# Unread products of a constant ahead of a sublayer's first products, and around a mixer's back-turn, in a two-part transformer block on one core

## The chip, the cores and the metric

The kernel runs on one core of one Trainium2 chip. The metric is device time in microseconds, the median of the runs shown.

## The reference

Two blocks follow each other on 256 tokens of width 1024, all in float32. The first has two layers of feed-forward, mixer, feed-forward; the second has two layers of attention and a routed mixture of experts. Every sublayer starts with a norm and a modulation of the tokens, and its first products need that result.

```python
def modulate(x, g_pre, shift, scale):
    return rms_norm(x, g_pre) * (1 + scale) + shift

for l in range(DEPTH):                       # DEPTH = 2, first block
    mod = (c_act @ ada_w[l] + ada_b[l]).reshape(bsz, N_SUB, 3, D_MODEL)[:, :, :, None, :]
    h = modulate(x, norm_pre[l, 0], mod[:, 0, 0], mod[:, 0, 1])
    x = residual_add(x, swiglu(h, ffn_w_gate[l, 0], ffn_w_up[l, 0], ffn_w_down[l, 0]), ...)
    h = modulate(x, norm_pre[l, 1], mod[:, 1, 0], mod[:, 1, 1])
    y = token_mixer(h, mix_w_in[l], ...)     # ends: merged = sum of gated branches; merged @ w_out
    x = residual_add(x, y, ...)
    h = modulate(x, norm_pre[l, 2], mod[:, 2, 0], mod[:, 2, 1])
    x = residual_add(x, swiglu(h, ffn_w_gate[l, 1], ...), ...)

for i in range(DEPTH):                       # second block
    h = rms_norm_2(x, norm_mix_g[i]) * (1.0 + sc1) + sh1
    y = diff_attention(h, ...) if i % 2 == 0 else chunked_attention(h, ...)
    x = x + g1 * y
    h = rms_norm_2(x, norm_ffn_g[i]) * (1.0 + sc2) + sh2
    x = x + g2 * grouped_moe(h, ...)
```

## The kernel before

Tokens lie on the 128 partitions in two tiles. A plan (`make_plan`) lists steps in order: norm, ffn or mixer or heads, resid, and in the mixers also backT and out. Each engine walks through the plan and issues its own instructions in the order in which the code stands; semaphores tie the engines together. TensorE's queue is in order, so what waits there holds everything behind it.

Weights arrive as chunks of 1 MB in a ring (`stage<-wstream`). ScalarE rounds each chunk to its high part (`w_hi`, L667), VectorE takes the rest (`w_lo`, L1181). A product in full precision is three matmuls (`mm3`, L1978, L1981, L1982): high by high, high by low, low by high, with 512 columns as a rule. The normed input is split in the same way into `hT_hi` and `hT_lo`.

A norm goes in four rounds, two for each token tile, and each handles half the width. For one round ScalarE scales the tokens (`tok`, L1087), TensorE transposes four blocks of 128 (`norm_round`, L1994) into one of two `tr` banks, VectorE applies the modulation (`tf`, L1838), ScalarE makes `hT_hi` (L1104) and VectorE makes `hT_lo` (L1847). A sublayer's first products are interleaved with the norm by `first_columns` (L2005): twelve matmuls of the first tile on the first half of the width, round 2's transposes, twelve on the second half, round 3's transposes, then twice twelve for the second tile. Rounds 0 and 1 stand before it in the queue. `first_columns` is called in seven places: in three feed-forwards (the second, third and fourth; they write to `gu`), in both mixers and in both heads sublayers (they write to `acc`; in the mixers with 416 columns). The first feed-forward does it another way.

At the end of a mixer the gated and summed branches lie in `tok`, tokens on partitions. The step backT turns them back: four calls of `turn` (L2076) with four transposes each, after a wait for VectorE's last sum (`mg_ready`, L1734). ScalarE (L745) and VectorE (L1207) copy each round's result into `hT_hi` and `hT_lo`, and rounds 2 and 3 wait until the banks of 0 and 1 are free. The step out multiplies by `w_out`.

`ident` is a 128x128 part of the table `const`, a constant in SBUF. `gu` (two banks), `acc` (four) and `tr` (two) are the PSUM banks.

Of the kernel before, what the change touches and what calls it, by code (L numbers as in the profile page):

```python
# [286 lines left out]
def build(nc, wstream, ada_stream, c_in, xin, const_in, vec_in, bgate_in, lam_in, rbias_in, t5_in, rel_in, rw_in, out):  # L287
# [14 lines left out]
    with ExitStack() as ctx:  # L302
        def sb(name, shape, dt=F32):
            return ctx.enter_context(nc.sbuf_tensor(name, shape, dt))
# [57 lines left out]
        const = sb("const", [P, N_CONST])  # L362
# [24 lines left out]
        acc = ctx.enter_context(nc.psum_tensor("acc", [P, 4, 512], F32))  # L387
        gu = ctx.enter_context(nc.psum_tensor("gu", [P, 2, 512], F32))
# [76 lines left out]
        def cst(name):  # L465
            return const[:, CONST[name][0]:CONST[name][1]]
# [36 lines left out]
        ident, ones, tri = cst("ident"), cst("ones"), cst("tri")  # L503
# [1471 lines left out]
        def _(pe):  # L1975
# [21 lines left out]
            def normed(b, part):  # L1997
# [4 lines left out]
                    pe.wait_ge(tr_free, b["u"] - 1 + part + 2 * t)  # L2002
                return ready

            def first_columns(b, dst, width=512):  # L2005

                for t in range(NT):
                    for part in range(2):
                        r = 2 * t + part
                        pe.wait_ge(tr_free, b["u"] - 1 + r)  # L2010
                        columns(b["n"] + part, dst, 4 * part, 4, part == 0, part == 1, width, only=(t,))
                        if t == 0:
                            norm_round(b["u"] - 4, b["tf"] - 4, 2 + part, b["src"] - 4)
# [53 lines left out]
            def turn(u, srcs, i=0, per=0, scaled=None):  # L2067

                if scaled is None:  # L2070
                    pe.wait_ge(tr_free, u + 1 + per * i)
                else:
                    pe.wait_ge(tf_ready, scaled)
                for j, src in enumerate(srcs):
                    rows_ = src.shape[-1]
                    ins = pe.transpose(tr[0:rows_, u % 2, j * P:(j + 1) * P], src, ident)  # L2076
                ins.then_inc(tr_full, 1)
# [566 lines left out]
            for step, b in plan:  # L2644
# [18 lines left out]
                elif kind == "mixer":  # L2663
                    mixer(b, step[1])
                elif kind == "backT":
                    pe.wait_ge(mg_ready, b["mg"])
                    for r in range(4):
                        turn(b["u"] + r, [tok[:, t, (2 * r + k) * P:(2 * r + k + 1) * P] for k in range(2) for t in range(NT)])
                elif kind == "out":
                    def of(c):  # L2670
# [16 lines left out]
                elif kind == "route":  # L2687
# [25 lines left out]
                    bank, sent, before = acc[:, 0, :], rt[:, 3, :], cst("before")  # L2713
# [180 lines left out]
```

## Time and profile before

| | us |
|---|---|
| median of 3 runs | 2193.05 |
| lowest, highest | 2189.24, 2195.68 |
| profiled execution | 2198.06 |
| its span, first to last instruction | 2196.2 |
| TensorE busy | 1993.8 |
| VectorE busy | 1423.0 |
| ScalarE busy | 841.4 |
| mean granted TensorE clock | 0.969 |

The profile is of one execution. A timeline row gives start, duration, engine, line and operation, output and inputs by their names, shapes, and in brackets the idle time before it and what ended it. Matmuls are pipelined: a row's end is later than the moment at which the next can start. The granted clock is a share of TensorE's full speed; it has two levels, 1.00 (2.4 GHz) and 0.50 (1.2 GHz). "issue" stands where the profile names no releaser.

### The profile page before, as it was taken

To read this page: it belongs to the slowest core of one execution; us is meant where nothing else is said; L and a number is where in the kernel's file an instruction comes from. 1 tells how busy PE (TensorE), PEld (TensorE's weight loads), DVE (VectorE), ACT (ScalarE), POOL (GpSimd) and SP (SyncE) were. 2 spreads that over 40 slices of the span, in tenths; PEclk is the share of its full clock that TensorE was granted. 3 is DMA by queue.
4 is the path that set the end of the run, shared out by engine and by line. 5 is a ranking of instruction groups with operands and counts; after the bars stand their busy time and mean duration, and the time that the engine had idled before them with its cause. 6 is when DMAs were issued, how large, how long until landed. Compare 5 with 4: busy or idle time off the path is not lost.

```text
span 2196.2 us, 26289 instructions
## 1 busy us (share of the span) xinstructions
PE 1993.8 (91%) x9588; PEld 1457.0 (66%) x9588; DVE 1423.0 (65%) x2167; ACT 841.4 (38%) x1101; POOL 65.2 (3%) x93
## 2 busy tenths in 40 slices
PE   3999899999999999899999999976899879879987
PEld 2788777777887788777777887755544347654432
DVE  6888787767888799677766888776311157642111
ACT  3333545655444444555655334542100035320000
POOL 0000000000000000000000000111000011000000
PEclk9999999999999999999999999997999989989999
DMA  9999454427996899453426897433799975359997
GB/s 396 363 364 361 163 189 155 145 96 296 359 375 243 321 369 380 165 181 141 168 96 249 347 374 293 151 127 109 288 422 422 421 316 183 99 200 410 420 421 310
DMA packets 98175, 597.87 MB, mean 272 GB/s; under 512 B 20240, under 2 KB 23696, under 8 KB 27408
## 3 DMA queue, kind: packets, MB, share of 16 engines
q1 hardware_dynamic: 91600, 585.18, 67.9%
q10 hardware_dynamic: 6464, 11.15, 1.5%
q8 instruction: 76, 1.25, 0.2%
q14 instruction: 35, 0.29, 0.0%
HBM read 595.21 MB, written 1.09 MB: 272 GB/s over the span
## 4 chain that ended last, share of the span: by engine, by line
PE 58%; DMA 15%; DVE 15%; ACT 5%; issue 5%; POOL 1%; SPq 1%; DVEq 0%; ACTq 0%; POOLq 0%
PE acc L1978 9%; PE acc L1982 9%; PE acc L1981 9%; PE gu L2327 8%; DMA proj<-ada_stream 7%; PE tr L2327 5%; DVE w_lo L1181 5%; DMA w_raw<-wstream 4%; PE gu L1978 4%; PE gu L1982 4%; PE gu L1981 4%; PE tr L2076 2%; PE acc L2327 2%; DMA stage<-wstream 2%; DVE proj L1239 2%
## 5 line engine op out<-in xcount | busy, mean ns | idle before, releaser
L1181 DVE TENSOR_TENSOR w_lo<-stage,w_hi 128x2048 fp32r<-128x2048 f32 x233 | 532.5, 2289 | 85.1 <-ACT w_hi L667 84.3
L667 ACT ACTIVATE w_hi<-stage 128x2048 fp32r<-128x2048 f32 x233 | 444.6, 1912 | 236.7 <-PE acc L1982 233.1
L1239 DVE SCALAR_TENSOR_TENSOR proj<-proj,c_row 128x1024 f32<-128x1024 f32 x240 | 291.9, 1220 | 56.5 <-DMA proj<-ada_stream 45.9
L1978 PE MATMUL acc<-w_hi,hT_hi 128*128 128x512 f32 (+1 forms) x736 | 307.5, 418 | 20.6 <-DVE hT_lo L1847 12.2
L1978 PE MATMUL gu<-w_hi,hT_hi 128*128 128x512 f32 x704 | 284.8, 404 | 21.3 <-DVE pair L1309 10.5
L1982 PE MATMUL acc<-w_hi,hT_lo 128*128 128x512 f32 (+1 forms) x736 | 292.7, 398 | 0.0
L1981 PE MATMUL acc<-w_lo,hT_hi 128*128 128x512 f32 (+1 forms) x736 | 292.6, 398 | 0.0
L1982 PE MATMUL gu<-w_hi,hT_lo 128*128 128x512 f32 x704 | 278.8, 396 | 0.0
L1981 PE MATMUL gu<-w_lo,hT_hi 128*128 128x512 f32 x704 | 278.5, 396 | 0.0
L1978 PE MATMUL acc<-w_hi,yT_hi 128*128 128x512 f32 (+1 forms) x460 | 181.3, 394 | 2.7 <-ACT proj L961 2.7
L1978 PEld LDWEIGHTS acc<-w_hi,hT_hi 128*128 128x128 f32 x736 | 143.3, 195 | 58.5 <-DVE hT_lo L1847 15.5
L1982 PE MATMUL acc<-w_hi,yT_lo 128*128 128x512 f32 (+1 forms) x460 | 179.3, 390 | 0.0
L1981 PE MATMUL acc<-w_lo,yT_hi 128*128 128x512 f32 (+1 forms) x460 | 179.1, 389 | 0.0
L2327 PE MATMUL gu<-stage,got 128*64 128x512 f32 x736 | 163.6, 594 | 14.7 <-DMA stage<-wstream 14.7
L1978 PEld LDWEIGHTS gu<-w_hi,hT_hi 128*128 128x128 f32 x704 | 134.8, 191 | 53.0 <-DVE pair L1309 13.0
L1982 PEld LDWEIGHTS acc<-w_hi,hT_lo 128*128 128x128 f32 x736 | 142.3, 193 | 30.7
L1981 PEld LDWEIGHTS acc<-w_lo,hT_hi 128*128 128x128 f32 x736 | 143.3, 195 | 25.7
L1982 PEld LDWEIGHTS gu<-w_hi,hT_lo 128*128 128x128 f32 x704 | 134.6, 191 | 29.5
L1981 PEld LDWEIGHTS gu<-w_lo,hT_hi 128*128 128x128 f32 x704 | 135.0, 192 | 26.7
L2327 PEld LDWEIGHTS gu<-stage,got 128*64 128x64 f32 x736 | 57.1, 137 | 117.5 <-issue 104.2
L1396 DVE TENSOR_TENSOR pair<-pair,gu 128x256 f32<-128x256 f32 x32 | 13.5, 421 | 169.6 <-ACT pair L806 169.6
L2327 PE MATMUL tr<-w_raw,hidT 128*64 128x512 f32 x512 | 114.3, 595 | 4.7 <-DVE got L1379 3.0
(230 smaller groups left out, 2278.7 us busy)
## 6 DMA issues: line engine op xcount, KB each, us to landing
stage<-wstream SPq DMA_DIRECT2D x332, 1024.0 KB, 5.9
proj<-ada_stream SPq DMA_DIRECT2D x120, 1024.0 KB, 7.8
w_raw<-wstream SPq DMA_DIRECT2D x96, 1024.0 KB, 16.7
tok<-gate_rows SPq DMA_DIRECT2D x10, 512.0 KB, 4.1
tf<-bgate_in ACTq DMA_DIRECT2D x12, 256.0 KB, 3.3
proj<-rel_in ACTq DMA_DIRECT2D x16, 192.0 KB, 2.4
z_mix<-wstream SPq DMA_DIRECT2D x2, 1024.0 KB, 17.6
once<-wstream SPq DMA_DIRECT2D x2, 1024.0 KB, 25.6
```

Source lines behind the costliest of these rows:

```text
L667: act.activation(w_hi[:, n % PARTS, :], stage[:, n % STAGES, :], ACT.Copy).then_inc(hi_ready, 1)
L1181: dve.tensor_tensor(w_lo[:, n % PARTS, :], stage[:, n % STAGES, :], w_hi[:, n % PARTS, :].bitcast(F32), ALU.subtract).then_inc(chunk_ready, 1)
L1239: ins = dve.scalar_tensor_tensor(w, w, 1.0, c_row[:], ALU.mult, ALU.mult, accum_out=dst)
L1396: dve.tensor_tensor(both[:, j, BLK:2 * BLK], both[:, j, 0:BLK], gu[:, j, BLK:2 * BLK], ALU.mult).then_inc(both_ready, 1)
L1978: ins = pe.matmul(dst, l_hi, r_hi, start=start, stop=False, skip_group_check=True)
L1981: pe.matmul(dst, l_hi, r_lo, start=False, stop=False, skip_group_check=True)
L1982: return pe.matmul(dst, l_lo, r_hi, start=False, stop=stop, skip_group_check=True)
L2076: ins = pe.transpose(tr[0:rows_, u % 2, j * P:(j + 1) * P], src, ident)
L2327: return pe.matmul(dst, lhs, rhs, start=start, stop=stop, skip_group_check=True)
```

## The change

A helper `unread` issues f32 matmuls of 128x512 with `ident` as the stationary and the first 512 columns of `const` as the moving operand. Their result is not read: the next real product into that bank starts it anew. Four stand in `first_columns`, before its first wait and into the bank of the second token tile. In backT two stand before the wait for the last sum, and two between rounds 1 and 2, all into `gu`.

```diff
+            def unread(bank, times):
+
+                for _ in range(times):
+                    pe.matmul(bank, ident, const[:, 0:512], start=True, stop=True, skip_group_check=True)
+
             def first_columns(b, dst, width=512):
 
                 for t in range(NT):
                     for part in range(2):
                         r = 2 * t + part
+                        if r == 0:
+                            unread(dst(1) if width == 512 else acc[:, 1, :], 4)
                         pe.wait_ge(tr_free, b["u"] - 1 + r)
                         columns(b["n"] + part, dst, 4 * part, 4, part == 0, part == 1, width, only=(t,))
                         if t == 0:
...
                 elif kind == "backT":
+                    unread(gu[:, 0, :], 2)
                     pe.wait_ge(mg_ready, b["mg"])
                     for r in range(4):
+                        if r == 2:
+                            unread(gu[:, 0, :], 2)
                         turn(b["u"] + r, [tok[:, t, (2 * r + k) * P:(2 * r + k + 1) * P] for k in range(2) for t in range(NT)])
```

In TensorE's queue the back-turn of a mixer stands as follows before. L1982 is the last product of the branches, `tr<-const,tok` are the transposes, the rows below belong to the step out.

```order
L1982 MATMUL acc<-w_hi,yT_lo 128x512
L2076 MATMUL tr<-const,tok 128x128 x16
L1978 MATMUL acc<-w_hi,hT_hi 128x512
L1981 MATMUL acc<-w_lo,hT_hi 128x512
L1982 MATMUL acc<-w_hi,hT_lo 128x512
```

In the same place after the change (lines are seven further down from `turn` on):

```order
L1982 MATMUL acc<-w_hi,yT_lo 128x512
L2008 MATMUL gu<-const 128x512 x2
L2083 MATMUL tr<-const,tok 128x128 x8
L2008 MATMUL gu<-const 128x512 x2
L2083 MATMUL tr<-const,tok 128x128 x8
L1978 MATMUL acc<-w_hi,hT_hi 128x512
```

The sixteen transposes are cut into two groups of eight with two products in front of each. At the start of the second feed-forward TensorE's queue holds, before (transposes of rounds 0 and 1, then the first products):

```order
L1982 MATMUL acc<-w_hi,hT_lo 128x512
L1994 MATMUL tr<-const,tok 128x128 x8
L1978 MATMUL gu<-w_hi,hT_hi 128x512
L1981 MATMUL gu<-w_lo,hT_hi 128x512
L1982 MATMUL gu<-w_hi,hT_lo 128x512
```

and after:

```order
L1982 MATMUL acc<-w_hi,hT_lo 128x512
L1994 MATMUL tr<-const,tok 128x128 x8
L2008 MATMUL gu<-const 128x512 x4
L1978 MATMUL gu<-w_hi,hT_hi 128x512
L1981 MATMUL gu<-w_lo,hT_hi 128x512
L1982 MATMUL gu<-w_hi,hT_lo 128x512
```

Only the four products are new there. The queues of the other engines hold the same rows in the same order as before.

## Rows read from the trace of the kernel before

**Rows 1.** The page: busy time of TensorE, share of the span, instructions.

```profile
PE 1993.8 (91%) x9588; PEld 1457.0 (66%) x9588; DVE 1423.0 (65%) x2167; ACT 841.4 (38%) x1101; POOL 65.2 (3%) x93
```

**Rows 2.** Waits of TensorE: waiting tile and line, releaser: us, times, longest.

```profile
PE acc L1978 <- DVE hT_lo L1847: 12.2, 8, 2.6
```

**Rows 3.** Timeline, TensorE: start, us, instruction, shapes; f32 products in the first mixer.

```profile
411.37 1.14 PE L2327 MATMUL acc<-soft_p,const 128*128 128x128 f32 x6
412.27 0.48 PE L1978 MATMUL acc<-w_hi,hT_hi 128*128 128x512 f32 x1
```

**Rows 4.** Chain of waits, second feed-forward: start, us, piece; the last pieces at each clock.

```profile
515.21 0.43 PE gu L1981
...
516.87 0.23 PE gu L1981
```

**Rows 5.** Timeline, TensorE: back-turns of both mixers, and the next norm after each.

```profile
481.21 1.09 PE L2076 MATMUL tr<-const,tok 128*128 128x128 f32 x8 [1.50 <-DVE tok L1734]
...
484.02 1.25 PE L2076 MATMUL tr<-const,tok 128*128 128x128 f32 x8 [1.71 <-DVE hT_lo L1207]
...
507.47 1.27 PE L1994 MATMUL tr<-const,tok 128*128 128x128 f32 x8 [0.40 <-ACT tok L1087]
...
1145.46 1.09 PE L2076 MATMUL tr<-const,tok 128*128 128x128 f32 x8 [1.51 <-DVE tok L1734]
...
1148.27 1.97 PE L2076 MATMUL tr<-const,tok 128*128 128x128 f32 x8 [1.71 <-DVE hT_lo L1207]
...
1174.31 1.27 PE L1994 MATMUL tr<-const,tok 128*128 128x128 f32 x8 [0.40 <-ACT tok L1087]
```

**Rows 6.** Busy time by stretch: PE, PEld, DVE, ACT, POOL; PEclk, DMA share, GB/s.

```profile
478.00:490.00 12.00, 8.78 (x46) 6.89 (x45) 9.54 (x10) 4.08 (x5) 0.00 (x0) 1.00 0.04 1
...
1147.30:1154.10 6.80, 5.83 (x18) 4.97 (x19) 4.29 (x6) 2.99 (x3) 0.00 (x0) 0.50 0.07 1
```

**Rows 7.** Timeline, TensorE, then ScalarE and VectorE: start of the second feed-forward.

```profile
511.43 0.47 PE L1978 MATMUL gu<-w_hi,hT_hi 128*128 128x512 f32 x1 [2.69 <-issue]
...
515.84 0.60 PE L1994 MATMUL tr<-const,tok 128*128 128x128 f32 x4
...
516.38 0.50 PE L1978 MATMUL gu<-w_hi,hT_hi 128*128 128x512 f32 x1
...
514.50 1.33 ACT L1087 ACTIVATE tok<-x_tok,rs 128x512 f32<-128x512 f32 x2
...
515.64 0.68 DVE L1847 TENSOR_TENSOR hT_lo<-tf,hT_hi 128x512 fp32r<-128x512 f32 x1
```

**Rows 8.** Timeline, TensorE, then VectorE: start of the third feed-forward.

```profile
708.61 0.76 PE L1978 MATMUL gu<-w_hi,hT_hi 128*128 128x512 f32 x1 [2.69 <-issue]
...
714.19 0.47 PE L1978 MATMUL gu<-w_hi,hT_hi 128*128 128x512 f32 x1
...
712.82 0.69 DVE L1847 TENSOR_TENSOR hT_lo<-tf,hT_hi 128x512 fp32r<-128x512 f32 x1
```

**Rows 9.** Timeline, TensorE, then VectorE: start of the first heads sublayer.

```profile
1379.14 0.58 PE L1978 MATMUL acc<-w_hi,hT_hi 128*128 128x512 f32 x1
...
1377.40 0.69 DVE L1847 TENSOR_TENSOR hT_lo<-tf,hT_hi 128x512 fp32r<-128x512 f32 x1
```

**Rows 10.** Timeline, TensorE: second column half in the first mixer.

```profile
248.06 0.46 PE L1978 MATMUL acc<-w_hi,hT_hi 128*128 128x416 f32 x1 [0.45 <-DVE hT_lo L1847]
```

**Rows 11.** Timeline, then the stretch: start of the second heads sublayer.

```profile
1787.57 1.97 PE L1994 MATMUL tr<-const,tok 128*128 128x128 f32 x8 [7.01 <-ACT tok L1087]
...
1791.95 0.80 PE L1978 MATMUL acc<-w_hi,hT_hi 128*128 128x512 f32 x1 [2.40 <-DVE hT_lo L1847]
...
1796.59 0.60 PE L1994 MATMUL tr<-const,tok 128*128 128x128 f32 x4
...
1782.00:1795.80 13.80, 5.82 (x17) 4.66 (x18) 10.49 (x18) 7.92 (x16) 3.92 (x4) 0.51 0.59 240
```

**Rows 12.** Chain of waits of the third feed-forward, 700 to 905 us, by line.

```profile
by line: DMA proj<-ada_stream 32.3%; DVE w_lo L1181 17.3%; issue 8.8%; DVE proj L1239 8.3%; PE gu L1978 4.8%; PE gu L1982 4.4%; PE gu L1981 4.4%; DVE pair L1309 1.8%; PE acc L1982 1.8%; PE acc L1981 1.8%; PE acc L1978 1.7%; ACT pair L718 1.
```

## The prediction

> **What bounds the kernel now.** I read the page first: TensorE is busy for 91% of the span [rows 1]. The reader is to see that little but TensorE's own queue can set the end, so a change inside that queue counts wherever no other engine was late. Second comes the list of waits: products of the next sublayer wait for the low part of their input, hT_lo, in eight waits of up to 2.6 us [rows 2], and the three later feed-forwards have a gap of the same kind, 2.69 us [rows 7, 8]. Third, the timeline and the busy time by stretch, with the granted clock: after such a gap the clock is often at the lower of its two levels, 1.2 instead of 2.4 GHz. There a product with 512 columns takes 0.43 us, at the higher level 0.23 us [rows 4].
>
> So each seam between sublayers may cost twice: the gap, and slow products behind it. The change puts products that nobody reads into the gap. Whether the second cost counts is read from what stands next in the queue, and from when its operands are ready.
>
> **What one unread product costs.** The trace has three f32 products with a constant at full width, 128, 256 and 128 columns, together 512. They appear as six instructions, and the next product starts 412.27 - 411.37 = 0.90 us after the first [rows 3]. So each product is two instructions, 0.45 us each for 512 columns, and the 0.90 us include picking up after a wait. Without that I take 0.43 us, 0.86 a product. The other end is two instructions at 0.23 us each, 0.46. Four products are then 3.4 us, between 1.8 and 3.6. At the lower clock a product takes 1.7 us. There are 7 x 4 + 2 x 4 = 36 of them, 31 us of TensorE in all; the question is how much lies in gaps. Nothing else moves on any engine, and there is no new wait and no new DMA.
>
> **The two back-turns.** This is the largest term. The same code runs in both mixers and the trace shows both outcomes. In the first the transposes start at 481.21 and the next norm's at 507.47, 26.26 us apart; in the second at 1145.46 and 1174.31, 28.85 us apart [rows 5]. The gaps in front are the same, 1.50 or 1.51 us and twice 1.71 us. What differs is the clock: 1.00 around the first, 0.50 for 6.8 us in the second [rows 6]. The second loses 2.6 us to it. Two unread products, 1.72 us, lie in each gap. A matmul's end in the timeline is later than the engine is free (1.14 us shown in rows 3, followed after 0.90), by some 0.15 us, so there is room for about 1.65 and 1.85 us, and what sticks out is under 0.1 us. With the queue filled the clock should stay up: **-2.6 us** in the second mixer, 0 in the first.
>
> Here a rule is weighed. Around 481 us TensorE had little but sixteen transposes for some 5 us, and the clock stayed at 1.00 [rows 5, 6]. The Trainium skill says otherwise (TensorE: Matmul & The Clock Gate, Part 4: PE-mode transpose): transposes don't count as work for the clock in the way products do. By it the first back-turn should have dropped as the second did, and the change would bring 2.6 us more, 2187.1 us. The row speaks against that, at least at this point, and the sum doesn't use it.
>
> **The second feed-forward.** Transposes end at 507.47 + 1.27 = 508.74 [rows 5], the engine is free at about 508.6; unread products fill it to 512.0, which is 0.6 us past the 511.43 at which the first real one started [rows 7]. Twelve products at 0.23 us reach 514.8. Then come transposes of the second token tile, whose first half ScalarE has ready at about 515.2 (two instructions from 514.50, 1.33 us), whatever TensorE does. They end at about 515.7, and the next twelve products need hT_lo at 515.64 + 0.68 = 516.32. Before, they started at 516.38 [rows 7], though most of the first twelve had run at the lower clock. So the delay and the saving both vanish in the wait for VectorE: **-0.05 us**. The fourth feed-forward repeats this pattern, 0.
>
> **The third feed-forward.** Here all twelve ran low. hT_lo was ready at 712.82 + 0.69 = 713.51 and the products started at 714.19 [rows 8]. With a high clock unread and real products are done at 705.8 + 3.4 + 2.8 = 712.0, so hT_lo is what comes last: **-0.65 us**.
>
> **The mixers.** At 248.06 TensorE already waited 0.45 us for hT_lo, after a stretch of slow products [rows 10]; the second mixer has the same pattern. Columns are fewer (416), and the 0.6 us of delay fits as well: 0.
>
> **The first heads sublayer.** hT_lo was ready at 1377.40 + 0.69 = 1378.09, the products started at 1379.14 [rows 9]: **-1.05 us**.
>
> **The second heads sublayer.** Here the change costs. The engine had been idle for 7.01 us and the transposes ran low; the stretch to 1795.8 has a clock of 0.51 [rows 11]. The unread products start at about 1789.4 and take 1.7 us each. Before, the clock came back 3.85 us after the first product (1791.95). If it comes back as long after the first unread one, at 1793.3, then 3.9 us of low clock do 1.95 us of work, 1.5 us are left, and the twelve real products end at 1797.6 instead of 1796.59: **+1.0 us**. If it comes back at 1795.8 as before, +2.3; if earlier, near 0.
>
> **Sum.** -2.6 - 0.05 - 0.65 - 1.05 + 1.0 = -3.35 us. Against the profiled execution (2198.06 us, of which the span is 2196.2) that is 2194.7. That execution is 5.0 us above the median of the three, 2193.05, and which seams fall low differs between executions: identical back-turns did in one profile. One of two back-turns in the profile is taken as the usual share, so the same sum stands against the median: **2189.7 us**, 0.15% less.
>
> **Rivals.** (1) *All low clock is on the path.* Twelve products lose 12 x 0.20 = 2.4 us at the lower clock, a back-turn 2.6. If all seams fell low and nothing else waited: 7 x 2.4 + 2 x 2.6 = 22 us, less 7 x 0.6 for what sticks out of the gaps, -18 us, 2175 us. For it: TensorE is busy 91%, and its queue feeds the whole feed-forward behind. Against it: the readiness of hT_lo in rows 7 and 10, which no clock moves. A mild form, where other executions have both back-turns low and more full losses at the feed-forwards, gives -7 to -9 us, 2184 to 2186 us.
> (2) *The unread products don't hold the clock*, because the clock falls on something else than an empty queue. Then only delays are left: 0.6 us at six places, swallowed by waits where a wait follows, +1 to +2 us at the second heads sublayer: 2193 to 2195 us. For it: nothing shows such products in the trace. Against it: in the second feed-forward the clock came back under a row of products after the gap, with nothing else changed [rows 4, 7].
> (3) *Slower: the unread products themselves run low.* The seven places then take 6.9 us instead of 3.4 in front of the twelve real products. At the second feed-forward 508.6 + 6.9 + 2.8 = 518.3 against 515.84, +2.5 us. It decides for the worse once it happens at about four of the seven, +10 against -3, 2200 us. Against it: where I looked, at six of the seven, the queue was full until some 0.4 us before the transposes [rows 5], and only the second heads sublayer starts low.
> (4) *The gain is given back.* The third feed-forward's chain runs for 32.3% through the modulation stream's DMAs [rows 12], so its 0.65 us may be lost; so may those before it, were the stream's order not tied to the chunks that TensorE frees. It gives 2190 to 2191 us and changes no sign.
>
> **How the numbers follow.** Within 0.3% means within 6.6 us, about what a measurement of this kernel can tell from no change. My forecast together with (4) has 0.60; (1) in either form 0.20; (2) 0.12; (3) 0.06; that an execution's mix of seams shifts the median up alone 0.02. Faster by over 0.3% needs less than 2186.5: case (1) and the lucky edge of the forecast, 0.22. Slower by over 0.3%: (3) and a little, 0.07. The rest, 0.71. The range runs from the mild form of (1), 2184, to the end of (2), 2195; it leaves out the full form of (1) and (3), under 2 in 10.
>
> **What will show it.** In the profile after, the unread products appear as 72 instructions, about 0.43 us apart. Back-turns to next norm: 26.3 us in both mixers, at a clock of 1.00. In the feed-forwards the first real product starts 0.6 us later after the transposes, and the second twelve start 0.05 us after hT_lo. The second heads sublayer shows unread products at half speed. I am wrong if a low stretch still follows the seams, or if the span falls by more than 7 us, for then the products behind hT_lo were not what I took them for.

## The result, and the profile after the change

| | before | after |
|---|---|---|
| median of 14 runs each | 2193.34 us | 2196.41 us |
| lowest, highest | 2188.96, 2196.99 | 2193.82, 2199.84 |
| profiled execution | 2198.06 us | 2197.49 us |

The changed kernel takes 1.0015 times the time of the kernel before, 95% interval 1.0008 to 1.0022. That is 3 us more, where 3.35 us less was forecast, and 2196.41 us lies above the end of the range, 2195. The change is within the 0.3% that were called no change. A second series of runs gave 1.0009 [1.0000, 1.0018]. The profiled execution of the kernel before is not one of the 14 and is longer than each of them.

The page of the kernel after the change, beside [rows 1] (busy us and instructions of each engine), and its line on the DMA queue q8 (packets, MB, share of the 16 DMA engines):

```profile
PE 2012.5 (92%) x9660; PEld 1459.3 (66%) x9660; DVE 1421.6 (65%) x2167; ACT 841.5 (38%) x1101; POOL 65.1 (3%) x93
...
q8 instruction: 77, 1.26, 0.2%
```

**The seams did what was forecast.** Timeline of TensorE after the change, both back-turns and the norm behind each, which answers to [rows 5]; then the stretch that answers to the second one of [rows 6] (PE, PEld, DVE, ACT, POOL busy, granted clock, DMA share, GB/s):

```profile
477.42 1.05 PE L2083 MATMUL tr<-const,tok 128*128 128x128 f32 x8
478.30 1.88 PE L2008 MATMUL gu<-const 128*128 128x512 f32 x4
480.18 1.25 PE L2083 MATMUL tr<-const,tok 128*128 128x128 f32 x8
503.62 1.27 PE L1994 MATMUL tr<-const,tok 128*128 128x128 f32 x8 [0.40 <-ACT tok L1087]
...
1145.74 1.05 PE L2083 MATMUL tr<-const,tok 128*128 128x128 f32 x8
1146.62 1.88 PE L2008 MATMUL gu<-const 128*128 128x512 f32 x4
1148.50 1.25 PE L2083 MATMUL tr<-const,tok 128*128 128x128 f32 x8
...
1171.95 1.27 PE L1994 MATMUL tr<-const,tok 128*128 128x128 f32 x8 [0.40 <-ACT tok L1087]
```

```profile
1147.30:1154.10 6.80, 6.80 (x31) 4.84 (x30) 4.91 (x6) 3.17 (x4) 0.00 (x0) 1.00 0.07 1
```

Back-turn to norm is 26.20 us in the first mixer and 26.21 in the second, where it was 26.26 and 28.85. The clock is 1.00 in that stretch.

**Where the time went instead** is seen when each stage is measured from the first transposes of its norm to those of the next (L1994; both profiled executions, us). In brackets stands the part up to the transposes of round 3, which I call the seam:

| stage | before | after | forecast | measured |
|---|---|---|---|---|
| first mixer | 268.32 | 268.22 | 0 | -0.10 |
| second feed-forward (to round 3) | 197.18 (11.78) | 198.48 (11.76) | -0.05 | +1.30 (-0.02) |
| third feed-forward (to round 3) | 198.78 (12.38) | 201.60 (11.79) | -0.65 | +2.82 (-0.59) |
| second mixer | 270.88 | 268.25 | -2.6 | -2.63 |
| fourth feed-forward (to round 3) | 194.93 (11.75) | 194.91 (11.79) | 0 | -0.02 (+0.04) |
| first heads (to round 3) | 161.06 (12.86) | 160.13 (11.78) | -1.05 | -0.93 (-1.08) |
| second heads (to round 3) | 149.56 (12.22) | 152.02 (12.61) | +1.0 | +2.46 (+0.39) |

Every seam in brackets is within 0.06 us of its forecast, but for the second heads sublayer, which the forecast made 0.6 us too dear. The loss lies behind the seams: late in the third feed-forward, and in the second heads sublayer. The second feed-forward's +1.30 does not come back when the changed kernel is profiled again (below).

The rows of the table add up to +2.9 us, but the two profiled executions differ by -0.6. The rest is mostly the first feed-forward, 209.77 us before and 205.96 after. No unread product stands in it or ahead of it, and over the fourteen profiled executions of this study whose start is not delayed and whose transfers are full it takes 206.0 to 209.8 us. What moves it is not known; it is one reason why the medians, and not the two profiles, say how much slower the kernel is.

### The profile page after: what moved, and what is told of

It is laid out like the page before. It is cut to its first block, busy times and chain, and to the rows that moved or that the text cites. A ratio compares the mean times of both kernels' runs of the same rounds, so it can differ in the third digit from the quotient of the medians.

```text
span 2195.7 us, 26433 instructions
## 1 busy us (share of the span) xinstructions
PE 2012.5 (92%) x9660; PEld 1459.3 (66%) x9660; DVE 1421.6 (65%) x2167; ACT 841.5 (38%) x1101; POOL 65.1 (3%) x93
## 3 DMA queue, kind: packets, MB, share of 16 engines
q8 instruction: 77, 1.26, 0.2%
## 4 chain that ended last, share of the span: by engine, by line
PE 60%; DMA 15%; DVE 14%; ACT 5%; issue 4%; POOL 1%; SPq 1%; DVEq 0%; ACTq 0%; POOLq 0%
PE acc L1978 9%; PE acc L1982 9%; PE acc L1981 9%; PE gu L2334 8%; DMA proj<-ada_stream 6%; PE tr L2334 5%; PE gu L1978 4%; DVE w_lo L1181 4%; DMA w_raw<-wstream 4%; PE gu L1982 4%; PE gu L1981 4%; PE tr L2083 3%; PE acc L2334 2%; DMA stage<-wstream 2%; DVE proj L1239 2%
## 5 line engine op out<-in xcount | busy, mean ns | idle before, releaser
L1982 PE MATMUL acc<-w_hi,hT_lo 128*128 128x512 f32 (+1 forms) x736 | 290.0, 394 | 0.0
L1982 PE MATMUL gu<-w_hi,hT_lo 128*128 128x512 f32 x704 | 276.0, 392 | 0.0
L1982 PE MATMUL acc<-w_hi,yT_lo 128*128 128x512 f32 (+1 forms) x460 | 178.8, 389 | 0.0
L1982 PEld LDWEIGHTS acc<-w_hi,hT_lo 128*128 128x128 f32 x736 | 140.6, 191 | 30.3
L1981 PEld LDWEIGHTS acc<-w_lo,hT_hi 128*128 128x128 f32 x736 | 141.4, 192 | 26.2 <-issue 1.0
L1982 PEld LDWEIGHTS gu<-w_hi,hT_lo 128*128 128x128 f32 x704 | 132.7, 189 | 28.8
```

Of the source, the lines that this page charges most:

```text
L1981: pe.matmul(dst, l_hi, r_lo, start=False, stop=False, skip_group_check=True)
L1982: return pe.matmul(dst, l_lo, r_hi, start=False, stop=stop, skip_group_check=True)
```

## First series: one part at a time

**Back-turns alone.** Against the kernel before:

```diff
                 elif kind == "backT":
+                    unread(gu[:, 0, :], 2)
                     pe.wait_ge(mg_ready, b["mg"])
                     for r in range(4):
+                        if r == 2:
+                            unread(gu[:, 0, :], 2)
```

> Only the two pairs of unread products in the two back-turns are left; none stands in front of a sublayer. Theory A (the back-turns gain 1 to 2.6 us as predicted, and the loss comes from the four products in front of sublayers): 0.5 to 2.6 us faster than the kernel before, ratio about 0.999. Theory B (the back-turns' gain is given back, since the stages behind them are paced by the modulation stream's DMAs and not by TensorE): ratio 1.000, with back-turns of 26.3 us in the profile all the same. Theory C (any unread product costs, wherever it stands, because the clock's extra time at 2.4 GHz is taken elsewhere): slower, 1.0005 or more.

Measured: 1.0037 [1.0023, 1.0051], slower than the whole change. The result is on the side of theory C only, but its reason is not seen: both back-turns take 26.2 us, and the time is lost in the fourth feed-forward, which nothing was added to and which takes 203.58 us.

**Feed-forwards alone.** `first_columns` issues its four products only where `ffn` calls it, and the back-turns have none:

```diff
-                first_columns(b, lambda t: acc[:, t, :])
+                first_columns(b, lambda t: acc[:, t, :], times=0)
...
-                first_columns(b, lambda t: acc[:, t, 0:PROJ_W - c0], PROJ_W - c0)
+                first_columns(b, lambda t: acc[:, t, 0:PROJ_W - c0], PROJ_W - c0, 0)
```

> Only the twelve unread products in front of the second, third and fourth feed-forward are left. Theory A (the loss is there: the products that pace the modulation stream are pushed together and two feed-forwards end on its DMAs): slower by 2 to 5 us, ratio 1.001 to 1.002, with more idle time of TensorE between 600 and 700 us and between 800 and 900 us. Theory D (the loss is at the second heads sublayer, where the clock is low): ratio 1.000 or a little below.

Measured: 1.0056 [1.0035, 1.0077]. That is more than either theory said. The fourth feed-forward is the long one again, 202.29 us.

**Mixers and heads alone.** The products only where the mixers and heads call it, and none in the back-turns:

```diff
-                    first_columns(b, lambda t: gu[:, t, :])
+                    first_columns(b, lambda t: gu[:, t, :], times=0)
```

> Only the sixteen unread products in front of both mixers and both heads sublayers are left. Theory D (unread products at the lower clock cost 1 to 4 us in front of the second heads sublayer, and the rest nothing): slower by 1 to 3 us, ratio 1.0005 to 1.0015. Theory A (loss in the feed-forwards): ratio 0.9995 to 1.000, with first real products of the second heads sublayer about 1 us later than before, those of the first 1 us earlier.

Measured: 1.0032 [1.0018, 1.0046], again more than either theory said. No stage of its profile explains it: the profiled execution, 2192.25 us, is the shortest of its 11, and the median is 9.2 us above. Its second heads sublayer takes 153.22 us.

**The kernel before, once more.**

> The kernel before, unchanged but for an empty line at its end: a second profile of it. Ratio 1.000. It shows how much the length of each stage varies from one execution to another with nothing changed; if the second and third feed-forward differ by 1 to 3 us from the first profile here too, the difference between the first two profiles there is no sign of the change.

Measured: 0.9992 [0.9977, 1.0007]. In its profile both back-turns run low (28.65 and 28.86 us).

No part is cheap, and the parts together would cost 1.2% where the whole costs 0.1 to 0.15%. Prices of parts that don't add up mean that something else than the parts' own work is priced.

## Second series: unread work away from the seams

**36 short products early.** Products of 16 columns, behind TensorE's wait for the first loads and ahead of the plan:

```diff
             pe.wait_ge(ld, 16 * N_LD)
+            for _ in range(36):
+                pe.matmul(gu[:, 0, 0:16], ident, const[:, 0:16], start=True, stop=True, skip_group_check=True)
```

> No unread product stands at a seam. 36 small ones (16 columns) stand at the very start, where TensorE waits for its first input until 29 us anyway; every later instruction of TensorE is thereby pushed down by 72 places, as in the changed kernel. Theory L (what costs is not when the products run but that the instructions behind them lie elsewhere in the program or its buffers elsewhere in memory, so that transfers that pace the feed-forwards land later): slower by 3 to 8 us, ratio 1.0015 to 1.004. Theory A or B (it is the products' time or the earlier start of the stages): ratio 1.000.

**36 short products at the end**, the same lines behind TensorE's last work.

> The same 36 small unread products behind TensorE's last real work, where it is idle for 12 us. The program is as long as the changed one, but nothing else is displaced. Theory L in the form 'length of the program': slower by 3 to 8 us, ratio 1.0015 to 1.004. Theory L in the form 'displaced instructions': ratio 1.000, while early36 is slower. All other theories: 1.000.

Measured: 1.0042 [1.0029, 1.0056] and 1.0047 [1.0034, 1.0061]. At first sight added instructions cost 0.4% wherever they stand. The timelines of TensorE, of the one with early and the one with late products, say otherwise:

```profile
25.78 15.54 PE L2645 MATMUL gu<-const 128*128 128x16 f32 x72 [25.78 <-DMA lam<-lam_in]
41.16 1.95 PE L1994 MATMUL tr<-const,tok 128*128 128x128 f32 x8
```

```profile
2185.56 15.54 PE L2722 MATMUL gu<-const 128*128 128x16 f32 x72 [2.17 <-issue]
```

Neither place is free. The 72 matmuls take 15.54 us, 0.216 us each, though they have 16 columns and not 512. The early ones start at 25.78 and push the first transposes from 29.4 to 41.16; at round 3 of the first norm 7.4 us of that are left (51.24 against 43.83 in the kernel before, once more). The late ones outlast VectorE's last sums, and the last stage is 9.0 us longer. Without these, the ratios are 1.0008 and 1.0006. I had called both places idle without reading how long the products stay there. What theory L forecast is not seen in either run.

**Shorter unread products** at all nine places of the changed kernel:

```diff
-                    pe.matmul(bank, ident, const[:, 0:512], start=True, stop=True, skip_group_check=True)
+                    pe.matmul(bank[:, 0:128], ident, const[:, 0:128], start=True, stop=True, skip_group_check=True)
```

> The changed kernel with every unread product cut from 512 to 128 columns: the same instructions in the same places, a quarter of the time (0.2 us each), so no real product is delayed. Theory L: as slow as the changed kernel, ratio 1.001 to 1.005. Theory E (TensorE's own time: the products stick out of the gaps by 0.6 us at seven places and more at the lower clock): ratio 0.999 to 1.000. If the clock is what matters, the mean granted clock is back at 0.970 with it.

Measured: 1.0006 [0.9997, 1.0015], between the two theories, with a mean clock of 0.973 and not 0.970. The third feed-forward is long here too, 198.97 us. Back-turns are at 26.28 us twice, so even these, which leave a gap of 1.75 us in front of a feed-forward's first product, keep the clock up. The second heads sublayer takes 149.35 us.

**The changed kernel, once more.**

> The changed kernel once more, beside the parts of it and on one chip with them. The parts alone gave 1.0032, 1.0037 and 1.0056 on one chip, the whole 1.0015 on another. If the cost is that of the chip's memory and the same for any variant (theory L), 1.003 to 1.006 here; if the parts' costs and gains add up, about 1.0015.

Measured: 1.0009 [1.0000, 1.0018]. The second feed-forward now takes 195.17 us, so its 198.48 was that execution's; the third takes 200.85, long again, the second heads sublayer 152.73. These two belong to the kernel.

## Third series: is it the modulation stream?

In a long feed-forward TensorE waits for VectorE, which waits for a transfer of the modulation stream. List of waits, third feed-forward (us in all, times, longest). VectorE's wait before the change:

```profile
DVE proj L1239 <- DMA proj<-ada_stream: 10.1, 8, 4.2
```

After the change, TensorE's waits for VectorE and then VectorE's for the stream:

```profile
PE gu L1978 <- DVE pair L1309: 2.8, 3, 1.4
PE tr L2083 <- DVE pair L1309: 2.7, 1, 2.7
PE acc L1978 <- DVE yT_lo L1314: 1.7, 1, 1.7
```

```profile
DVE proj L1239 <- DMA proj<-ada_stream: 18.6, 10, 6.1
```

**Thin transfers, kernel before.** In the feed-forwards' loops a transfer of the stream brings 16 of 128 partitions (128 KB; the expectation's "64 KB or so" was a slip), and the column sums work on old data, scaled by 0.2. The kernel leaves out the true values of the modulation. Lines cut at "...":

```diff
+                if isinstance(i, int):
...
+                else:
+                    sp.dma_start(ada_stage[0:16, q, :], ada_stream[at].rearrange("a p c -> (a p) c")[0:16, :]).then_inc(
+                        ada_landed[q], 16)
...
-                ins = dve.scalar_tensor_tensor(w, w, 1.0, c_row[:], ALU.mult, ALU.mult, accum_out=dst)
+                ins = dve.scalar_tensor_tensor(w, w, 1.0 if isinstance(i, int) else 0.2, c_row[:], ALU.mult, ALU.mult, accum_out=dst)
```

> The kernel before, with thin transfers of the modulation stream: in the feed-forwards' loops each transfer brings 16 of the 128 partitions (64 KB or so in place of 1 MB), and the column sums that use them work on old data scaled by 0.2, so the modulation's values are not the reference's; the instructions and their order are the same. Theory S (the changed kernel saves 3.3 us at the seams and loses it in the feed-forwards, because L1239 waits for transfers of the modulation stream that land late, and TensorE then waits for VectorE): the second, third and fourth feed-forward, first transpose of a norm to first transpose of the next, take 195.0 to 195.3 us each in place of 197.18, 198.78 and 194.93, the gaps in front of L1239 sum to under 3 us in each, and the whole is 2 to 6 us shorter than the kernel before on the same chip (ratio 0.997 to 0.999). Rival L (the stream is not the cause; what the feed-forwards lose comes from elsewhere): a feed-forward of 197 us or more is still seen, ratio 1.000.

**Thin transfers, changed kernel**, the same edit.

> The changed kernel with the same thin transfers and the same loss of the modulation's values. Theory S: with no late transfer left, the gain at the seams stays: 3.3 us less than the thin kernel before, so a ratio 0.0015 lower than that one's (0.9955 to 0.9975), and feed-forwards of 195.0 to 195.3 us, less 0.65 in the third if its start gains. Rival L (the added instructions cost time wherever they stand, whatever the stream does): a feed-forward of 198 us or more as in the changed kernel (third: 201.60 and 200.85), and a ratio at or above that of the thin kernel before.

Measured: 0.9984 [0.9970, 0.9997] without the change and 0.9987 [0.9977, 0.9997] with it. The third feed-forward falls from 200.85 or 201.60 to 195.34 us with the change, and from 198.78 or 195.79 to 194.97 without it. So the stream carries this stage's loss. But the two ratios are alike, where theory S wanted the changed one 0.0015 lower: a second loss must stand outside the stream. The profiles show where it can be: the second heads sublayer takes 150.33 us without the change and 153.05 with it.

**Back-turns alone and feed-forwards alone, once more.**

> The kernel with the two and two products in the back-turns alone, once more, on another chip, to see whether its long fourth feed-forward (203.58 us, and 195.2 in the second and 195.85 in the third) belongs to the kernel or to the one execution that was profiled. Theory S with transfers that come late by chance: the long feed-forward is another one or none, each within 195 to 202 us, and the ratio comes out anywhere from 0.9985 to 1.004. Rival F (the late transfer is fixed by the program's timing): the fourth again takes 202 to 205 us and the ratio is 1.003 to 1.004 again.

> The kernel with the four products in front of the second to fourth feed-forward alone, once more. It gave 1.0056 with a fourth feed-forward of 202.29 us. By chance: the fourth is within 195 to 198 us this time or the long one is elsewhere, ratio 0.999 to 1.005. Rival F (fixed): the fourth takes 201 to 204 us again, ratio 1.005 to 1.006.

Measured: 1.0037 [1.0023, 1.0051] again, with a fourth feed-forward of 199.01 us, and 1.0042 [1.0026, 1.0057], with 204.19 us in the third and 200.25 in the fourth. The place is mostly fixed, which is what F said, but the amount isn't, and 199.01 and 200.25 lie under F's bounds. And the third feed-forward of the second kernel was 195.06 us in one execution and 204.19 in the other.

## Fourth series: the place of the instruction pieces

What the long stages have in common is not seen in any engine's row. It is in q8. I took the start of each of its packets from the first transposes of the stage on. In the changed kernel's third feed-forward one comes at 81.6 us, in the two executions above at 88.8 us (195.06 us) and at 84.3 us (204.19 us). The order of instructions ahead of a stage decides where a piece ends, so each kernel, and each number of added instructions, has its own places. By the Trainium skill (Advanced Engine Details and Errata, ISA Cache) a line of the cache that holds an engine's instructions is 16 KB, 256 instructions. The trace agrees as to size: 77 packets are 1.26 MB. TensorE's 9660 matmuls and as many weight loads would fill 75.5 such pieces, so q8 is taken to be TensorE's queue. The next experiments move the pieces with empty instructions; those that stand behind the wait for the first loads can also delay the start, so that is read off each time.

**48 empty instructions in the kernel before**, behind the wait for the first loads (`pad` is a semaphore that nothing waits for):

```diff
             pe.wait_ge(ld, 16 * N_LD)
+            for _ in range(48):
+                pe.nop().then_inc(pad, 1)
```

> The kernel before with 48 empty instructions in TensorE's stream at the program's start, where TensorE is idle until 29 us; no product is added. They shift the places at which TensorE's 16 KB pieces of instructions are fetched by some 5 us to earlier. Theory I (a piece fetched 81 to 84 us after a feed-forward's start makes a transfer of the modulation stream late, and the stage never recovers): the third and the fourth feed-forward have a fetch at 81 to 85 us and take 197 to 204 us each in place of 195.8 to 198.8 and 194.9, and the whole is 5 to 12 us slower (1.002 to 1.005). Rival N (the matmuls that were added cost the time, not the place of the fetches): stages as in the kernel before, ratio 0.999 to 1.001.

Measured: 1.0055 [1.0042, 1.0068]. No product is added and nothing of the start is lost (round 3 of the first norm at 43.45 us, 43.83 or 43.86 without), yet the third feed-forward takes 200.67 us and the fourth 201.98. Both are in the forecast's bounds, and the ratio is a little above them. Wait of VectorE for the stream in this fourth feed-forward (us in all, times, longest); in the kernel before it was 4.2 us, 7 times, at most 1.1:

```profile
DVE proj L1240 <- DMA proj<-ada_stream: 13.5, 8, 7.8
```

The forecast came out, but not by its reason, that a transfer is late at 81 to 84 us and the stage never recovers. The transfer in flight when the piece starts at 83.0 us lands 1.6 us later than in the kernel before (9.8 us after its issue against 8.2), but the next one takes 7.7 us against 8.1, and the stage does recover. From 100 us on both kernels issue the stream's transfers at the same times to 0.9 us, the last one at 167.6 and 167.7 us, and TensorE's products start at the same times, to 0.1 us, until 180 us. Only then do they fall behind, by 7.1 us at 190 us. The wait of 7.8 us is for that last transfer, and the next packet of q8 starts 2.0 us after its issue. DMA issues from 1341 to 1345 us, before (name, count, KB, us to landing):

```profile
proj<-ada_stream SPq DMA_DIRECT2D x1, 1024.0 KB, 8.1
```

and with the 48 empty instructions, with the line of q8 (packets, MB, share):

```profile
q8 instruction: 1, 0.02, 1.5%
proj<-ada_stream SPq DMA_DIRECT2D x1, 1024.0 KB, 15.6
```

So the piece at 81 to 85 us is a sign of a later one, some 87 to 93 us on, that falls into the stage's last transfer. The table at the end of the fifth series takes this up for all stages.

**144 empty instructions in the kernel before**, as many as the change adds.

> The kernel before with 144 empty instructions at the program's start, as many as the change adds. Theory I: the fetches stand at 72 to 74 us in the third and fourth feed-forward, as with the 36 short products at the start (196.4 and 196.1 us), so the stages take 195 to 196.5 us and the ratio is 0.999 to 1.001. Rival B (more instructions are slower wherever they stand, as the 36 short products at the start and at the end seemed to say, 1.0042 and 1.0047): ratio 1.003 to 1.005.

Measured: 1.0070 [1.0053, 1.0088], but again the place wasn't idle: the empty instructions hold the first transposes until 48.21 us, and 14.9 us of that stay at round 3. Without them the ratio is 1.0002, as theory I has it. The third and fourth feed-forward take 194.98 and 195.50 us, with pieces at 73.2 and 71.8 us, as theory I said.

**64 empty instructions in the changed kernel.**

> The changed kernel with 64 empty instructions at the program's start. Theory I: the fetch in the third feed-forward moves from 81.6 us to 74 to 76 us after its start, the stage takes 195.0 to 196.5 us in place of 200.85 to 201.60, and the ratio falls from 1.0009 to 1.0015 to 0.998 to 0.9995; the second heads sublayer keeps its 152 to 153 us. Rival N (the unread products themselves cost the third feed-forward): it stays at 199 to 202 us and the ratio at 1.001. The fourth feed-forward's fetch lands near 69 us, where no run has shown it; if that place is bad too, the fourth is long instead.

Measured: 1.0015 [1.0006, 1.0023]; 2.5 us of it is the start. Even without them, 1.0004, the ratio misses theory I's 0.998 to 0.9995, though the stages obey it. The third feed-forward takes 196.17 us with its piece at 74.6 us. The fourth, at 69.8 us, has 196.86.

**The changed kernel without the four products ahead of the second heads sublayer.**

```diff
-                first_columns(b, lambda t: acc[:, t, :])
+                first_columns(b, lambda t: acc[:, t, :], times=0 if hd is BAND else 4)
```

> The changed kernel without the four unread products in front of the second heads sublayer (32 products stay). Theory P (with the four there, the clock falls for 3.4 us more at 107 us and for 6.8 us at 124 us behind the sublayer's first transposes, in all four traces that have the four products and in one of nine that have not): these two falls are gone, the sublayer takes 149.4 to 150.5 us in place of 152.0 to 152.7, the third feed-forward stays at 198.9 to 201.6, and the ratio falls by 0.001 to 0.9999 to 1.0005. Rival Q (the falls come by chance or with the other products): 152 to 153 us, ratio 1.001.

Measured: 1.0015 [1.0006, 1.0025]. The profile shows what P said: 150.19 us in place of 152.0 to 152.7, and the third feed-forward at 201.34. Two stretches of the second heads sublayer, 107 and 124 us behind its first transposes, of the kernel before, after, and this one (us, PE busy, granted clock, DMA share, GB/s):

```profile
1894.50:1898.10 3.60, 3.59 (x17) 0.54 0.19 55
1911.70:1918.50 6.80, 6.80 (x36) 1.00 0.31 98
```

```profile
1891.40:1898.30 6.90, 6.90 (x26) 0.51 0.19 57
1908.50:1915.40 6.90, 6.18 (x22) 0.51 0.01 2
```

```profile
1890.10:1893.60 3.50, 3.50 (x16) 0.51 0.21 56
1907.20:1914.00 6.80, 6.80 (x37) 1.00 0.32 101
```

With the four products the clock stays low 3.4 us longer in the first stretch and falls once more in the second, a hundred microseconds behind them. Of the twenty profiled executions of this study, all six with four full products there have both and take 152.0 to 153.8 us. Of the other fourteen, one has both (the feed-forwards alone, once more: 153.05 us), and thirteen take 149.3 to 151.2. The median didn't fall with the stage here, though: 1.0015 is the changed kernel's ratio too, and P's 0.9999 to 1.0005 is missed.

## Fifth series: both causes taken away

**40 empty instructions in the changed kernel**, this time ahead of the wait for the first loads, where they cost nothing (round 3 at 42.66 us):

```diff
+            for _ in range(40):
+                pe.nop().then_inc(pad, 1)
             pe.nop().then_inc(pe_used, PARTS)
             pe.wait_ge(ld, 16 * N_LD)
```

> The changed kernel with 40 empty instructions at the very start of TensorE's stream, ahead of its wait for the first loads, which ends at 25.8 us, so that they cost nothing. Theory I: the fetch in the third feed-forward comes 76 to 78 us after its start and the stage takes 195.0 to 196.5 us in place of 200.85 to 201.60, the fourth has it at 70 to 72 us and takes 194.9 to 197, and the whole is 4 to 5 us shorter than the changed kernel: ratio 0.998 to 0.9995, faster than the kernel before. Rival G (the gains at the seams are no gains over many executions, since in the kernel before the clock falls there only in some of them): ratio 1.000 to 1.001 even with both feed-forwards at 195 us.

**The same without the four products ahead of the second heads sublayer.**

> The same without the four unread products in front of the second heads sublayer. Theory I with P: 1.0 to 2.5 us less than with them, the second heads sublayer at 149.4 to 150.5 us in place of 152 to 153.8, ratio 0.997 to 0.999. Rival Q (the sublayer's length in one execution is chance): the same ratio as with them, within 0.0007.

Measured: 1.0014 [1.0004, 1.0024] and 0.9993 [0.9979, 1.0006]. The stages of the first came out as theory I has them: 195.00 and 195.68 us with pieces at 76.9 and 71.3, and VectorE's wait in the third feed-forward is

```profile
DVE proj L1240 <- DMA proj<-ada_stream: 7.9, 9, 1.6
```

in place of 18.6. But its profiled execution, 2193.25 us, is the shortest of its 11, and the median is 4 us above. What the others lose no trace shows, and the ratio misses the forecast of 0.998 to 0.9995. It is nearer to rival G (1.000 to 1.001), whose reason was not tested by itself. The second kernel's ratio is 0.0021 below the first's on the same chip (the medians are 2.5 us apart, 0.0011, and the intervals overlap), with 150.68 against 153.36 us in the second heads sublayer, as P had it. Its third feed-forward takes 196.72 us. It is the best version of the changed kernel that moves all its data, and it can't be told from the kernel before.

**All feed-forwards together.** The eighteen profiled executions with full transfers have 54 feed-forwards (second to fourth), sorted here by whether a q8 packet starts 81 to 85 us behind the stage's first transposes:

| piece at 81 to 85 us | stages | median | lowest, highest | over 196.5 us |
|---|---|---|---|---|
| yes | 12 | 201.1 us | 196.85, 204.19 | 12 |
| no | 42 | 195.2 us | 194.89, 198.78 | 5 |

The twelve come from ten executions of seven kernels, and three of these kernels have nothing added in the stage in question. The bounds of 81 to 85 us were drawn after nine of the twelve had been seen. The other three were forecast, and so were five stages of the runs with 144, 64 and 40 empty instructions that lie outside them (194.98 to 196.17 us).

The same 54 stages, sorted by whether a q8 packet starts within 6 us after the issue of the stage's last transfer of the modulation stream:

| piece 0 to 6 us into the last transfer | stages | the transfer lands after | stage: lowest, highest |
|---|---|---|---|
| yes | 11 | 13.0 to 15.6 us | 198.97, 204.19 |
| no | 43 | 6.9 to 12.3 us (42 of them up to 10.8) | 194.89, 198.78 |

This split leaves no overlap. The twelfth stage of the first table, 196.85 us, goes to the other side: its packet starts 6.4 us after the issue, and the transfer lands after 7.3 us. In the changed kernel's two executions the packet starts 0.3 and 0.6 us after the issue, and the transfer takes 13.7 and 13.0 us. Counted product by product against the fourth feed-forward of the kernel before, TensorE is 1.9 and 0.0 us late at 180 us, and 6.6 and 5.9 at 190. This split too was drawn afterwards, and no run moves the later piece without the earlier one.

## Why the prediction failed, point by point

- **The price of a product, the gaps.** Right: 72 instructions, a gap of 1.7 us filled by 1.88 us shown, and transposes that follow without a wait.
- **What bounds the kernel.** Right at the seams. It was wrong that little but TensorE's own queue can set the end: in the third feed-forward a transfer does.
- **The back-turns, -2.6.** Right in size and in the one-of-two share, which rested on two back-turns only and was lucky to that extent: of 20 back-turns without products in ten executions 11 have a low stretch, and the mean excess over 26.2 us is 1.3 us, 2.5 for both. With products 0 of 20 have one (26.19 to 26.28 us). The rule of the Trainium skill that was weighed, that transposes don't count as work for the clock in the way products do (TensorE: Matmul & The Clock Gate, Part 4: PE-mode transpose), was set aside on the strength of one row. More rows say that around the same sixteen transposes the clock falls in 11 cases and holds in 9; so one row could not decide, and the rule alone doesn't say which case comes.
- **Second and fourth feed-forward, mixers, first heads.** Right to 0.1 us at their seams, in the profiled pair. Against the median the sum took half of the back-turns' loss but all of the other low stretches, as if these came each time. Without the products the first heads' seam is long (12.80 or 12.86 us against 11.8) in only 2 of 11 executions and the third feed-forward's (12.38 to 12.61) in 4 of 10, so -1.05 was worth -0.2 on the mean and -0.65 was worth -0.3. The second feed-forward and the two mixers, put at 0.05 us or nothing, gain 0.2, 0.1 and 0.3. Together these seams were put at -1.75 us and gain 1.1 on the mean.
- **Third feed-forward, -0.65.** The seam was right in the profiled pair (-0.59); the stage lost 2.8 and, against the kernel before once more, 5 to 6 us. The step that failed is the sentence that nothing else moves on any engine, with no new DMA. The added instructions move the ends of all pieces that TensorE fetches; up to the start of this stage's products there are 64, enough to shift one from 89 to 81.5 us, and the piece after the next from 174.7 to 170.8 us, into the stage's last transfer of the modulation stream, which then lands after 13.7 us. Rival 4 named the right stage and the right wait, but only as a way to lose the 0.65 us again; it has no term by which the stage gets longer than before.
- **Second heads, +1.0.** Mis-sized, in two ways that differ in sign: the seam costs 0.39, and two clock falls far behind it some 2 more. At the seam the clock was back 2.9 us after the first unread product (1786.24 us in the profile after), not 3.9. The step looked at the first 14 us only. In the changed kernel's two profiles the stage is 2.5 and 3.2 us over the first profile of the kernel before, and 0.8 and 1.5 over the second; the median of the six executions with the products is 2.8 us over that of the fourteen without.
- **Sum.** On the mean the seams and back-turns give -3.6 us (-2.5 for the back-turns, -1.1 for the rest); the second heads sublayer takes back 2.8 and the third feed-forward 3 to 6. That is about +2 to +5, an estimate from single executions, and +2 and +3 us were measured. That these two losses are the whole of it isn't shown: with both removed the ratio is 0.9993 with an interval of 2.9 us to either side, which holds the seams' gain and also none.
- **Range.** Its upper end was that of the rival in which unread products do nothing. No bound was given for costs outside the sum, although the chain of [rows 12] has a third of a stage on a transfer with no slack.

**Open.** A packet of q8 holds one of the 16 DMA engines for about 0.95 us. Why it makes the stage's last transfer 5 to 7 us later, and other transfers of the stage by much less, is not shown. How four products keep the clock low a hundred microseconds later is open too. And one profiled execution is a poor witness of a median: the median is 9.2 us above it for the mixers and heads alone, 5.1 above for the feed-forwards alone and 3.1 to 4.1 above in four runs more, and 2.4 to 7.1 us below it in three. With both causes taken away in the profile, the median is still that of the kernel before and not under it, and what it loses is unknown.

## What to carry to other kernels

In this kernel, filling a queue's gap with unread products held the clock at the seam and gained what the rows around the seam say. Count only low stretches that nothing else hides, and count how often they come over several executions. But the added instructions also moved the places where later instructions are fetched, and where a transfer had no slack that cost as much as the gain. So read the instruction queue's packets against the transfers that pace a stage, and try the same change with some empty instructions in idle time before judging it. And a control that adds work in "idle" time must itself be read in the trace: three controls here cost 7, 9 and 15 us at the place where they stood.

## What the runs showed of the hardware

- 48 empty instructions, at no cost where they stand, made a kernel of 2194 us 0.55% slower [0.42, 0.68].
- When an instruction packet started 0.3 to 5.6 us into the last 1 MB transfer of a stage, the transfer took 13.0 to 15.6 us (11 of 11); otherwise 6.9 to 12.3 (43).
- Instructions for TensorE arrive in 16 KB packets, 76 in the kernel, mostly 20 to 32 us apart in a feed-forward, with one space of some 60; 48 instructions move them by 5.5 us (88.5 to 83.0 us in the fourth).
- An instruction of an f32 product takes 0.43 us with 512 columns and 0.11 us with 128 at a clock of 1.00 (eight in 1.06 us as shown, end included). With 16 columns it takes 0.216 us at 0.50 (the 72 at the end), twice the 0.11, so fewer columns than 128 gained nothing. Each loads 128 columns of weights anew, which is the likely bound and not shown to be.
- Four 128-column products in a feed-forward's gap held the clock as well as four of 512, with 1.75 us of the gap left open.
- An empty instruction that raises a semaphore takes 0.16 us: 48, 64 and 144 of them, from 25.8 us on, put the first transposes at 33.22, 35.70 and 48.21 us.
